# A decay recurrence, its output projection and its group norm put in another order, by halves of the rows

## The chip, the cores and the metric

The kernel runs on one core of one Trainium2 chip. The metric is the time on the device of one execution, in microseconds. The program has five engines with a queue each: PE (TensorE, matmuls), DVE (VectorE), ACT (ScalarE), POOL (GpSimd) and SP (SyncE, which here issues the weight transfers). They meet only in semaphores.

## The reference

Two blocks are computed for 256 rows of 1024 columns. The change lies in the middle of the second one, in a group of eight heads of 64 columns (RWKV-7). Cut to what matters:

```python
def rwkv7_scan(r, decay, k, v, kk, a):
    def step(S, inp):
        r_t, w_t, k_t, v_t, kk_t, a_t = inp
        sa = jnp.einsum('bhij,bhj->bhi', S, -kk_t)
        S = (S * w_t[:, :, None, :] + sa[..., None] * (kk_t * a_t)[:, :, None, :]
             + v_t[..., None] * k_t[:, :, None, :])
        y = jnp.einsum('bhij,bhj->bhi', S, r_t)
        return S, y
...
    y = rwkv7_scan(rh, heads(decay), kh, vh, kk, ah)
    mean = jnp.mean(y, axis=-1, keepdims=True)
    var = jnp.mean(jnp.square(y - mean), axis=-1, keepdims=True)
    y = (y - mean) * lax.rsqrt(var + GN_EPS)
    y = y * lnx_w + lnx_b
    y = (y + bonus) * g
...
    return jnp.concatenate([y_rwkv, y_att], axis=-1) @ w_out
```

The result is added to the rows, normalized, and goes into a feed-forward block.

## The kernel before, in words

The order on every engine is written out by hand. `plan()` only gives each product a PSUM bank (eight banks; `s.use(name, bank)`) and lists the weight units. A weight unit is 1 MB; SP loads it, ACT writes its high part (`split` in ACT's block), DVE its low part, and PE multiplies in three matmuls (`three`): high by high, high by low, low by high. Three units can be split at a time, so the split of a unit waits until PE is done with the one three before. On PE, `take(name)` waits for the bank to be empty and `give(ins, name)` reports it full.

The scan is done in 8 rounds (`NCH`) of 32 rows (`C`). Ahead of it an inverse is computed for four groups `g` of four heads and 128 rows (`INVERSE`; steps GN to ZZ, two groups taking turns); its step Z1 multiplies the inverse with two matrices, `An` and `Z[:, 1]`, 64 columns each.

A round c on PE: `recalled` (the state against WT, 8 matmuls into two banks, one for even heads and one for odd), the state product of Kn and Vn (8 matmuls), one of eight groups of masked products (`PRODUCTS`, four matmuls of heads of one parity; they are for the outputs only), then, once DVE has written SA, the state product of Bn and SA. Even and odd heads have a state bank each (`ste`, `sto`). DVE in a round: decays the old state, one instruction for each parity (64 partitions each); writes SA, one each; adds the new state, one each; masks the 512 columns of products. The next round's `recalled` waits for the new state.

Behind the eight rounds PE computes the outputs of rows 0 to 127 (`y0`) and of rows 128 to 255 (`y1`), each from SA products, Vn products and states. Then comes the group norm of all 256 rows: means (`gm0`, `gm1`, by halves of the columns), DVE's centring, ACT's squares, sums over each head (`gv`), ACT's root, DVE's reciprocal, `unfold_rows` which spreads it to the columns again, and four DVE steps with a copy on ACT between. The output projection has four units: 512 attention rows of `w_out` by 512 columns, twice (48 matmuls of 128x512), and 512 RWKV rows by 512 columns, twice (48 more). The attention half does not need the scan, and PE runs it while DVE and ACT work at the group norm. `row_transposes` then turns the new rows for the feed-forward block.

Lines of the profile: L1967 is `recalled`, L1961 the state products, L1982 the masked products, L2001 and L2011 the outputs, L2017 the means, L1837 the variance, L1847 the unfolding, L1607 to L1609 the three matmuls of `three`, L1708 the row transposes; L1918 to L1932 are the inverse. On DVE L1416 is the decay, L1423 SA, L1429 the state's addition, L1362 a mask, L1441 the centring, L1447 the reciprocal, L1457 to L1466 the four steps, L999 a low part of weights, L1224 the residual. On ACT L613 is a copy out of PSUM, L873 the squares, L875 the root, L880 the high part of the rows, L602 that of weights.

## Time and profile before

| | |
|---|---|
| time of 3 runs, median (lowest, highest) | 1093.39 us (1091.84, 1093.6) |
| the profiled execution | 1094.86 us |
| its span in the trace | 1093.1 us |
| mean granted clock of PE | 0.943 of 2.4 GHz |
| PE busy | 1000.1 us, 91% |
| DVE busy | 580.9 us, 53% |
| ACT busy | 452.9 us, 41% |
| the chain that ended last | PE 85%, DVE 5%, issue 5%, ACT 3% |

The span is the time from the first to the last recorded instruction. Busy is the time in which an engine ran something; a wait for a semaphore is not busy. The record of a matmul contains its way through the array, so in a row of them the distance between starts is what each costs, and "mean ns of one" is longer. An fp32 matmul stands as two records. "128\*64" behind MATMUL is the part of the array that is used, rows by columns. PEclk (granted clock) is 1.00 at 2.4 GHz and 0.50 at 1.2 GHz. In an idle note, [1.01 <-DVE ...] is how long the engine stood still before the group's first instruction, and who released it.

### The profile page before, as it was taken

The page shows a single profiled execution, that of the slowest core. Times are in us where ns is not written, and L with a number is a line of the kernel's source. Part 1 is how long each engine was busy: PE and PEld are TensorE (multiplying, and loading weights), DVE is VectorE, ACT ScalarE, POOL GpSimd, SP SyncE. Part 2 cuts the span into 40 slices and gives each one's busy share as a digit, 9 for nine tenths or more (in the row PEclk, how much of TensorE's full clock was granted, in tenths as well). Part 3 has the DMA queues.
Part 4 walks back from the last instruction along what each step waited for, and adds up shares of the span by engine and source line. Part 5 has one row for each costly group of instructions (what it writes and reads, how often), then busy time and mean ns, then how long its engine had stood idle before and what let it go on. Part 6 is the DMA issues. An engine that isn't in the chain of part 4 may idle for free.

```text
span 1093.1 us, 16977 instructions
## 1 busy us (share of the span) xinstructions
PE 1000.1 (91%) x7278; PEld 889.5 (81%) x7278; DVE 580.9 (53%) x711; ACT 452.9 (41%) x620; POOL 42.9 (4%) x86
## 2 busy tenths in 40 slices
PE   4999999998899995998899999999889589999996
PEld 4898788897698784997778999998877369998995
DVE  4456656456545478344437555556533286555554
ACT  5445554444444563221035444444432255444442
POOL 6000000000110002100000000000100000000000
PEclk9999999999989897897599999999999889999998
DMA  9663344455556231000014565656556145565530
GB/s 307 196 196 118 125 145 135 136 185 183 182 174 184 86 116 39 2 1 1 1 40 150 197 193 174 200 170 199 167 160 176 27 135 165 182 195 191 193 116 39
DMA packets 108714, 152.52 MB, mean 140 GB/s; under 512 B 4050, under 2 KB 86368, under 8 KB 108640
## 3 DMA queue, kind: packets, MB, share of 16 engines
q1 hardware_dynamic: 101120, 141.45, 40.0%
q10 hardware_dynamic: 5296, 4.79, 1.9%
q0 software_dynamic: 2224, 5.20, 1.5%
q8 instruction: 58, 0.95, 0.4%
q14 instruction: 16, 0.13, 0.0%
HBM read 145.58 MB, written 1.06 MB: 134 GB/s over the span
## 4 chain that ended last, share of the span: by engine, by line
PE 85%; DVE 5%; issue 5%; ACT 3%; DMA 1%; POOL 0%; POOLq 0%; SPq 0%; ACTq 0%; DVEq 0%
PE banks L1607 22%; PE banks L1608 22%; PE banks L1609 22%; PE banks L1932 4%; PE banks L2069 3%; PE banks L1982 1%; PE banks L1961 1%; ACT wh L602 1%; PE banks L1736 1%; PE banks L1725 1%; PE banks L1719 1%; PE banks L1718 1%; DMA raw<-in_w_in 1%; PE banks L1967 1%; PE banks L1867 1%
## 5 line engine op out<-in xcount | busy, mean ns | idle before, releaser
L999 DVE TENSOR_TENSOR wl<-raw,wh 128x2048 fp32r<-128x2048 f32 x132 | 302.2, 2291 | 213.7 <-ACT wh L602 212.8
L1607 PE MATMUL banks<-xh,wh 128*128 128x256 f32 x1216 | 345.5, 284 | 2.0 <-DVE xl L1047 1.8
L1608 PE MATMUL banks<-xl,wh 128*128 128x256 f32 x1216 | 342.5, 282 | 0.0
L1609 PE MATMUL banks<-xh,wl 128*128 128x256 f32 x1216 | 342.2, 281 | 0.0
L602 ACT ACTIVATE wh<-raw 128x2048 fp32r<-128x2048 f32 x132 | 252.1, 1911 | 126.0 <-PE banks L1609 121.9
L1607 PEld LDWEIGHTS banks<-xh,wh 128*128 128x128 f32 x1216 | 230.6, 190 | 8.5 <-issue 7.2
L1608 PEld LDWEIGHTS banks<-xl,wh 128*128 128x128 f32 x1216 | 230.3, 189 | 1.3
L1609 PEld LDWEIGHTS banks<-xh,wl 128*128 128x128 f32 x1216 | 230.6, 190 | 0.0
L1607 PE MATMUL banks<-wh,yh 128*128 128x512 f32 x288 | 113.2, 393 | 1.8 <-DVE yl L1466 1.8
L1608 PE MATMUL banks<-wl,yh 128*128 128x512 f32 x288 | 112.2, 390 | 0.0
L1609 PE MATMUL banks<-wh,yl 128*128 128x512 f32 x288 | 112.2, 390 | 0.0
L896 ACT ACTIVATE ytmp<-banks 128x512 f32<-128x512 f32 x32 | 19.1, 598 | 110.1 <-PE banks L1609 110.1
L1607 PEld LDWEIGHTS banks<-wh,yh 128*128 128x128 f32 x288 | 54.1, 188 | 13.0 <-issue 2.8
L1609 PEld LDWEIGHTS banks<-wh,yl 128*128 128x128 f32 x288 | 54.1, 188 | 11.5
L1479 DVE TENSOR_TENSOR ytmp<-ytmp 128x512 f32<-128x512 f32 x32 | 22.2, 693 | 77.5 <-ACT yh L900 77.5
L1608 PEld LDWEIGHTS banks<-wl,yh 128*128 128x128 f32 x288 | 54.1, 188 | 10.3 <-issue 0.2
L613 ACT ACTIVATE arena<-banks 128x512 f32<-128x512 f32 (+1 forms) x51 | 29.7, 593 | 78.2 <-PE banks L1609 40.2
L1607 PE MATMUL banks<-wh,xh 128*128 128x512 f32 x112 | 47.7, 426 | 13.3 <-DVE xl L1559 7.8
L1608 PE MATMUL banks<-wl,xh 128*128 128x512 f32 x112 | 46.5, 415 | 0.0
L1609 PE MATMUL banks<-wh,xl 128*128 128x512 f32 x112 | 46.2, 412 | 0.0
L2069 PE MATMUL banks<-arena,yover 128*32 128x256 f32 x512 | 31.9, 412 | 12.3 <-issue 12.3
L1607 PEld LDWEIGHTS banks<-wh,xh 128*128 128x128 f32 x112 | 22.6, 202 | 19.9 <-issue 14.6
(289 smaller groups left out, 1115.8 us busy)
## 6 DMA issues: line engine op xcount, KB each, us to landing
raw<-in_l_ffn_up SPq DMA_DIRECT2D x32, 1024.0 KB, 5.5
raw<-in_l_ffn_down SPq DMA_DIRECT2D x32, 1024.0 KB, 5.0
raw<-in_w_in SPq DMA_DIRECT2D x29, 1024.0 KB, 5.3
raw<-in_l_w_in SPq DMA_DIRECT2D x13, 1024.0 KB, 5.2
raw<-in_l_pw SPq DMA_DIRECT2D x12, 1024.0 KB, 5.4
arena<-arena ACTq DMA_DIRECT2D x64, 71.0 KB, 3.0
raw<-in_w_out SPq DMA_DIRECT2D x4, 1024.0 KB, 5.1
raw<-in_l_w_out SPq DMA_DIRECT2D x4, 1024.0 KB, 5.0
```

Of the source, the lines that this page charges most:

```text
L602: nc.scalar.activation(wh[:, u % WBUFS, :], raw[:, u % RAWS, :], ACT.Copy).then_inc(E("hi_split"), 1)
L613: nc.scalar.activation(dst, src, ACT.Copy, scale=scale).then_inc(empty(name), 1)
L896: nc.scalar.activation(ytmp[:, k % 2, :], bank(name), ACT.Relu).then_inc(empty(name), 1)
L999: nc.vector.tensor_tensor(wl[:, u % WBUFS, :], raw[:, u % RAWS, :], wh[:, u % WBUFS, :].bitcast(F32), ALU.subtract).then_inc(E("lo_split"), 1)
L1479: mark(nc.vector.tensor_tensor(hid, hid, hid, ALU.mult))
L1607: mm(out, hh, mh, start=start, stop=False)
L1608: mm(out, hh, ml, start=False, stop=False)
L1609: return mm(out, hl, mh, start=False, stop=stop)
L1718: mm(out[:, 0:P], q[:, 0:P], k[:, 0:P], start=True, stop=True)
L1719: give(mm(out[:, P:384], q[:, P:T], k, start=True, stop=True), f"sc{a}")
L1932: ins = mm(o, m(ts[lhs]), m(ts[rhs]), start=True, stop=True)
L2069: ins = mm(out[32 * q:32 * q + 32, j * T:(j + 1) * T], tap_blocks(i)[:, g, 4 * j + q, :], shifted(i)[:, j, q, SHIFTS * g:SHIFTS * g + T], ...
```

## The change

1. The two halves of the state are written into one bank (`st`), and DVE decays and adds them in one instruction each.
2. The masked products are taken in another grouping: in a round four heads, even and odd by turns (`received`), into two banks; DVE masks them in two instructions ahead of the state's addition.
3. In rounds 0 to 3, PE does six matmuls of the first attention unit at the end of a round (`attention_part`). In round 4 it does the states' part of `y0`, in rounds 5 and 6 its two products' parts.
4. The group norm is done for rows 0 to 127 first and for the others behind it, and the projection too: `rwkv_part(c, s)` is 12 matmuls for one half of the rows and of the columns.
5. `An` moves to where `Z[:, 0]` lies, and Z1 is one matmul of 128 columns instead of two of 64.
6. ACT's split of the last projection unit stands ahead of the copy of `y0`.

The core of the diff (some removed lines left out; the code before is above):

```diff
     for c in range(NCH):
         s.use(f"sae{c}", 2), s.use(f"sao{c}", 3)
         if c < NCH - 1:
...
+            s.use(f"st{c}", 1)
+        s.use(f"pre{c}", 0), s.use(f"pro{c}", 7)
+        if c == 0:
+            s.unit("N", "l0_w_out_2", 512, 0, None)
+            s.unit("N", "l0_w_out_2", 512, 512, None)
+            s.use("wp0_0", 4), s.use("wp0_1", 5)
+        elif c == 4:
+            s.use("y0", 6)
+    s.use("gm0", 6)
+    s.use("y1", 1)
+    s.use("gv0", 2)
+    s.use("wp1_0", 6)
+    s.use("gv_b0", 3)
+    s.use("gm1", 0)
+    s.use("wp1_1", 7)
+    s.use("gv1", 2)
+    s.use("gv_b1", 3)
     for c in range(2):
         s.unit("N", "l0_w_out_2", 0, 512 * c, f"wp{c}_1")
 
...
-        An, Bn, Kn, Vn = tiles(slot(8)), tiles(slot(3)), tiles(slot(10)), tiles(slot(11))
+        Bn, Kn, Vn = tiles(slot(3)), tiles(slot(10)), tiles(slot(11))
         Z = oslot(0, 2).rearrange("p (w s h d) -> p w s h d", w=2, s=NT, h=8)
+        An = Z[:, 0, :, :, :].rearrange("p s h d -> p s (h d)")
...
             for i in range(2):
                 copy_out(WT[:, :, i * P:(i + 1) * P], f"wt{i}")
 
...
             next_unit()
...
+            copy_out(YT[:, :, half(0)], "y0")
+            group_squares(0)
+            copy_out(YT[:, :, half(1)], "y1")
+            group_deviation(0)
+            group_squares(1)
+            group_deviation(1)
+            for t in range(NT):
+                act.wait_ge(E("rwkv_out"), t + 1)
+                nc.scalar.activation(yh[:, 0:4, half(t)], centred[:, :, half(t)], ACT.Copy).then_inc(E("rwkv_hi"), 1)
             for _ in range(2):
                 next_unit()
 
...
             for c in range(NCH):
...
+                    if c:
+                        wait_empty(dve, f"st{c - 1}")
+                    mark(nc.vector.tensor_tensor(heads_of(decayed), heads_of(S(c)), pc1, ALU.mult))
...
+                for par in range(2):
+                    use = f"sa{'eo'[par]}{c}"
+                    wait_full(dve, use)
+                    nc.vector.tensor_tensor(heads_of(SA[pb:pb + C, tt, :])[:, par::2, :], heads_of(bank(use)[pb:pb + C, 0:T]),
+                                            Z[pb:pb + C, 1, tt, par::2, :], ALU.add).then_inc(empty(use), 1)
+                upto = const("upinc32").rearrange("p (o t) -> p o t", o=1).broadcast_to([P, 2, P])
+                for par in range(2):
+                    use = f"pr{'eo'[par]}{c}"
+                    wait_full(dve, use)
+                    at = 512 * (c // 2 % 2) + T * (c % 2)
+                    nc.vector.tensor_tensor(products(2 * tt + par)[:, at:at + T].rearrange("p (h t) -> p h t", h=2),
+                                            bank(use)[:, 0:T].rearrange("p (h t) -> p h t", h=2), upto, ALU.mult)\
+                        .then_inc(empty(use), 1)
                 if c < NCH - 1:
...
+                    wait_full(dve, f"st{c}")
+                    sync()
+                    nc.vector.tensor_tensor(S(c + 1), bank(f"st{c}")[:, 0:T], decayed, ALU.add).then_inc(empty(f"st{c}"), 1)
...
+            centre(0)
             next_unit()
+            group_rstd(0)
             dve.wait_ge(E("gates_folded"), 4)
...
+            normalize(0)
+            centre(1)
+            gate_and_shift(0)
+            group_rstd(1)
+            rwkv_low(0)
+            normalize(1)
+            gate_and_shift(1)
+            rwkv_low(1)
             add_residual("wp", units=((), (2,)), norm="f0")
             split_norm("f0", (2, 3))
             next_unit()
...
                             elif name == "Z1":
-                                mm(o[:, 0:HD], m(ts[4]), An[:, tt, h * HD:(h + 1) * HD], start=True, stop=True)
-                                ins = mm(o[:, HD:P], m(ts[4]), Z[:, 1, tt, h, :], start=True, stop=True)
+                                ins = mm(o.rearrange("p (w d) -> p w d", w=2), m(ts[4]), Z[:, :, tt, h, :],
+                                         start=True, stop=True)
...
+            def attention_part(c, s, ks):
+
+                u = UID[("N", "l0_w_out_2", 512, 512 * c)]
+                if s == 0 and ks[0] == 0:
+                    arrived(u)
+                h, l = w_views(u, 512)
+                out = take(f"wp{c}_{s}") if ks[0] == 0 else bank(f"wp{c}_{s}")
+                rows = slice(s * P, (s + 1) * P)
+                for k in ks:
+                    ins = three(out, yh[:, 4 + k, rows], yl[:, 4 + k, rows], h[:, k, :], l[:, k, :], k == 0, False)
+                if s == 1 and ks[-1] == 3:
+                    ins.then_inc(E("unit_summed"), 1)
+
...
+                    ins = three(bank(f"wp{c}_{s}"), yh[:, k, rows], yl[:, k, rows], h[:, k, :], l[:, k, :], False, k == 3)
+                give(ins, f"wp{c}_{s}")
...
+            def first_half_outputs(c):
+                if c == 4:
+                    take("y0")
+                    state_part(0, 0, 4, True)
+                elif c == 5:
+                    product_part(0, SA, 0, False)
+                else:
+                    give(product_part(0, Vn, 512, True), "y0")
+
...
+                def received(p, par):
+                    h = 4 * (c % 2) + 2 * p + par
+                    return mm(outs[par][:, p * P:(p + 1) * P], htile(kTil if c // 2 % 2 else bTil, tt, h), htile(rTil, tt, h),
+                              start=True, stop=True)
+
+                if c:
+                    wait_empty(pe, f"st{c - 1}")
                 outs = [take(f"sa{e}{c}") for e in "eo"]
                 for par, ins in enumerate(both_parities(recalled)):
                     give(ins, f"sa{'eo'[par]}{c}")
                 if c < NCH - 1:
-                    take(f"ste{c}"), take(f"sto{c}")
+                    take(f"st{c}")
                     both_parities(state_mm(Kn, Vn, True))
...
+                outs = [take(f"pr{e}{c}") for e in "eo"]
+                for par, ins in enumerate(both_parities(received, 2)):
+                    give(ins, f"pr{'eo'[par]}{c}")
+                if c < NCH - 1:
+                    wait_empty(pe, f"sae{c}"), wait_empty(pe, f"sao{c}")
+                    give(both_parities(state_mm(Bn, SA, False))[1], f"st{c}")
+                if c < 4:
+                    attention_part(0, c // 2, range(2 * (c % 2), 2 * (c % 2) + 2))
+                elif c < NCH - 1:
+                    first_half_outputs(c)
+
...
+            group_mean(0)
+            take("y1")
+            state_part(1, 0, 4, True)
             wait_empty(pe, f"sae{NCH - 1}"), wait_empty(pe, f"sao{NCH - 1}")
...
+            product_part(1, SA, 0, False)
+            wait_empty(pe, f"pre{NCH - 1}"), wait_empty(pe, f"pro{NCH - 1}")
+            give(product_part(1, Vn, 512, True), "y1")
+            group_variance(0)
+            attention_part(1, 0, range(4))
+            unfold_group(0)
+            group_mean(1)
+            attention_part(1, 1, range(4))
+            group_variance(1)
+            rwkv_part(0, 0)
+            unfold_group(1)
+            rwkv_part(1, 0)
+            rwkv_part(0, 1)
             row_transposes("f0", "wp", 0)
-            nat_unit(("wp1_0", "wp1_1"), 0, yh, yl, turn=1, part=1)
+            rwkv_part(1, 1)
             row_transposes("f0", "wp", 1)
```

On PE, the end of a round and the start of the next, before. L1961 is the state product, L1967 `recalled`, L1982 the masked products; "x7" is seven more of the same:

```order
L1961 MATMUL banks<-arena 64x64 [waits emptied3,emptied2]
L1961 MATMUL banks<-arena 64x64 x7
L1967 MATMUL banks<-extra_t,arena 32x64 [waits emptied2,emptied3,emptied7,emptied4]
L1967 MATMUL banks<-extra_t,arena 32x64 x7
L1961 MATMUL banks<-arena 64x64 [waits emptied7,emptied4]
L1961 MATMUL banks<-arena 64x64 x7
L1982 MATMUL banks<-arena 128x128 [waits emptied0]
L1982 MATMUL banks<-arena 128x128 x3
```

The same place now (end of round 0, start of round 1). L2048 is the state product, L2054 `recalled`, L1641 to L1643 are the three matmuls of a weight unit, here of the attention half:

```order
L2048 MATMUL banks<-arena 64x64 [waits emptied3,emptied2]
L2048 MATMUL banks<-arena 64x64 x7
L1641 MATMUL banks<-wh,yh 128x512 [waits emptied4,lo_split,hi_split]
L1642 MATMUL banks<-wl,yh 128x512
L1643 MATMUL banks<-wh,yl 128x512
L1641 MATMUL banks<-wh,yh 128x512
L1642 MATMUL banks<-wl,yh 128x512
L1643 MATMUL banks<-wh,yl 128x512
L2054 MATMUL banks<-extra_t,arena 32x64 [waits emptied3,emptied2,emptied1]
L2054 MATMUL banks<-extra_t,arena 32x64 x7
L2048 MATMUL banks<-arena 64x64 [waits emptied1]
L2048 MATMUL banks<-arena 64x64 x7
```

Six matmuls of 128x512 have come between the second state product and the next `recalled`.

On ACT, from the copies of WT to the high part of the projection's rows, before. L613 is a copy out of PSUM, L873 the squares, L875 the root, L602 a split of weights:

```order
L613 ACTIVATE arena<-banks 128x4x128 [waits filled1]
L613 ACTIVATE arena<-banks 128x4x128 [waits filled0]
L613 ACTIVATE ytmp<-banks 128x4x128 [waits filled5]
L613 ACTIVATE ytmp<-banks 128x4x128 [waits filled6]
L873 ACTIVATE arena<-arena 128x512 [waits emptied1]
L873 ACTIVATE arena<-arena 128x512 [waits emptied0]
L875 ACT_TABLE_LOAD
L875 ACTIVATE arena<-banks,small 128x256 [waits filled1]
L602 ACTIVATE wh<-raw 128x2048 [waits unit_summed,unit_loaded3]
L880 ACTIVATE yh<-arena 128x512 [waits rwkv_out] x2
```

Now (L622 copy, L611 split of weights, L884 squares, L888 root, L899 high part of the rows):

```order
L622 ACTIVATE arena<-banks 128x4x128 [waits filled1]
L622 ACTIVATE arena<-banks 128x4x128 [waits filled0]
L611 ACTIVATE wh<-raw 128x2048 [waits unit_summed,unit_loaded3]
L622 ACTIVATE ytmp<-banks 128x4x128 [waits filled6]
L884 ACTIVATE yover<-yover 128x4x128 [waits emptied6]
L622 ACTIVATE ytmp<-banks 128x4x128 [waits filled1]
L888 ACT_TABLE_LOAD
L888 ACTIVATE thb<-banks,small 128x128 [waits filled2]
L884 ACTIVATE yover<-yover 128x4x128 [waits emptied0]
L888 ACTIVATE thb<-banks,small 128x128 [waits filled2]
L899 ACTIVATE yh<-yover 128x4x128 [waits rwkv_out] x2
```

The split of weights has moved up; the copy of `y1` stands ahead of the first root, and the second root ahead of the high part of the first rows.

On DVE, from the centring to the low parts, before (L1441 centring, L1447 reciprocal, L999 split of weights, L1457 to L1466 the four steps):

```order
L1441 SCALAR_TENSOR_TENSOR arena<-banks,ytmp 128x512 [waits filled1,emptied5,emptied6]
L1441 SCALAR_TENSOR_TENSOR arena<-banks,ytmp 128x512 [waits filled0]
L1447 RECIPROCAL arena<-arena 128x256 [waits emptied1,emptied0]
L999 TENSOR_TENSOR wl<-raw,wh 128x2048 [waits unit_summed,hi_split]
L1457 TENSOR_TENSOR arena<-arena,banks 128x512 [waits filled0,gates_folded]
L1457 TENSOR_TENSOR arena<-arena,banks 128x512 [waits filled1]
L1460 TENSOR_TENSOR arena<-arena 128x512 [waits emptied0]
L1460 TENSOR_TENSOR arena<-arena 128x512 [waits emptied1]
L1463 TENSOR_TENSOR arena<-arena,over 128x512 [waits dve_steps]
L1463 TENSOR_TENSOR arena<-arena,over 128x512
L1466 TENSOR_TENSOR yl<-arena,yh 128x512 [waits rwkv_hi] x2
```

Now (L1463 centring, L1017 split of weights, L1470 reciprocal, L1476, L1482 and L1484 the steps, L1489 the low part):

```order
L1463 SCALAR_TENSOR_TENSOR yover<-banks,ytmp 128x4x128 [waits emptied6,filled6]
L1017 TENSOR_TENSOR wl<-raw,wh 128x2048 [waits unit_summed,hi_split]
L1470 RECIPROCAL thb<-thb 128x128 [waits emptied2]
L1476 TENSOR_TENSOR yover<-yover,banks 128x4x128 [waits emptied6,filled3,gates_folded]
L1463 SCALAR_TENSOR_TENSOR yover<-banks,ytmp 128x4x128 [waits emptied1,filled0]
L1482 TENSOR_TENSOR yover<-yover,arena 128x4x128 [waits emptied3]
L1484 TENSOR_TENSOR yover<-yover,over 128x4x128 [waits dve_steps]
L1470 RECIPROCAL thb<-thb 128x128 [waits emptied2]
L1489 TENSOR_TENSOR yl<-yover,yh 128x4x128 [waits rwkv_hi]
L1476 TENSOR_TENSOR yover<-yover,banks 128x4x128 [waits emptied0,filled3]
L1482 TENSOR_TENSOR yover<-yover,arena 128x4x128 [waits emptied3]
L1484 TENSOR_TENSOR yover<-yover,over 128x4x128 [waits dve_steps]
```

The second reciprocal stands ahead of the first low part, and everything has 128 rows instead of half of the columns.

## Rows read from the trace of the kernel before

**Rows 1.** PE, timeline of rounds: start, length, line, shape, count, [idle before].

```profile
499.62 0.64 PE L1967 MATMUL banks<-extra_t,arena 64*32 64x64 f32 x16 [0.78 <-ACT arena L613]
500.19 0.68 PE L1961 MATMUL banks<-arena 32*64 32x64 f32 x16
500.80 1.16 PE L1982 MATMUL banks<-arena 64*128 64x128 f32 x8
...
509.74 1.07 PE L1967 MATMUL banks<-extra_t,arena 64*32 64x64 f32 x16 [1.01 <-DVE extra_t L1429]
...
511.78 2.07 PE L1982 MATMUL banks<-arena 64*128 64x128 f32 x8
...
515.90 1.07 PE L1967 MATMUL banks<-extra_t,arena 64*32 64x64 f32 x16 [1.01 <-DVE extra_t L1429]
```

**Rows 2.** PE, timeline of outputs, group norm and projection.

```profile
549.50 1.97 PE L2001 MATMUL banks<-arena 128*64 128x128 f32 x32
...
551.40 2.06 PE L2011 MATMUL banks<-arena,over 64*64 64x32 f32 x64
...
557.36 0.39 PE L1607 MATMUL banks<-wh,yh 128*128 128x512 f32 x1
557.59 0.39 PE L1608 MATMUL banks<-wl,yh 128*128 128x512 f32 x1
...
558.81 0.64 PE L1837 MATMUL banks<-arena,cst 128*32 128x256 f32 x8
559.38 0.50 PE L1607 MATMUL banks<-wh,yh 128*128 128x512 f32 x1
...
559.72 0.39 PE L1608 MATMUL banks<-wl,yh 128*128 128x512 f32 x1
...
571.40 0.47 PE L1607 MATMUL banks<-wh,yh 128*128 128x512 f32 x1 [1.78 <-DVE yl L1466]
...
584.86 0.36 PE L1607 MATMUL banks<-xh,wh 128*128 128x256 f32 x1
```

**Rows 3.** DVE, timeline at the end of a round.

```profile
508.76 0.88 DVE L1429 TENSOR_TENSOR extra_t<-banks,thb 64x256 f32<-64x256 f32 x2 [3.01 <-PE banks L1961]
...
509.67 0.69 DVE L1362 TENSOR_TENSOR arena<-banks,cst 128x512 f32<-128x512 f32 x1
```

**Rows 4.** Windows: busy us of PE, PEld, DVE, ACT, POOL, then PEclk; two of PE alone.

```profile
510.00:520.00 10.00, 8.99 (x98) 7.81 (x93) 4.92 (x12) 0.00 (x0) 0.00 (x0) 0.50 0.01 2
...
550.00:560.00 10.00, 9.26 (x119) 6.79 (x116) 1.38 (x2) 3.83 (x6) 0.00 (x0) 1.00 0.01 2
...
570.00:580.00 10.00, 8.60 (x39) 7.13 (x40) 5.29 (x6) 4.86 (x4) 0.00 (x0) 1.00 0.14 51
...
503.00:504.00 1.00, 0.43 (x9) 0.79 0.00 0
...
547.00:548.00 1.00, 1.00 (x20) 0.53 0.00 0
```

**Rows 5.** PE, timeline at the end of the inverse.

```profile
485.63 2.90 PE L1932 MATMUL banks<-arena 128*128 128x128 f32 x24
...
490.03 0.39 PE L1928 MATMUL banks<-over,arena 128*128 128x64 f32 x2
490.25 0.39 PE L1927 MATMUL banks<-arena 128*128 128x64 f32 x2
```

**Rows 6.** PE, timeline where products of one and of the other row half meet.

```profile
429.35 0.27 PE L1920 MATMUL banks<-over,arena 64*128 64x128 f32 x1
429.35 0.27 PE L1918 MATMUL banks<-over,arena 64*128 64x128 f32 x1
```

**Rows 7.** ACT and DVE, timeline of the group norm and the projection.

```profile
557.56 1.28 ACT L875 ACT_TABLE_LOAD   x1
...
560.13 1.75 DVE L1447 RECIPROCAL arena<-arena 128x256 f32<-128x256 f32 x1 [3.25 <-ACT arena L875]
...
577.76 2.29 DVE L999 TENSOR_TENSOR wl<-raw,wh 128x2048 fp32r<-128x2048 f32 x1
```

213 lines of the change are left out of this document (89 added, 124 removed).

## The prediction

> **What bounds the kernel now.** I read the page first (section 1: PE busy for 91% of the span; section 2: slices 16 to 20 carry a lowered PEclk, almost no DMA and a quiet ACT), then the windows of that stretch, its timeline engine by engine, and the chain of waits. The stretch is the part that the change rewrites: from the first matmul of the recurrence at 499.62 [rows 1] to the first up-projection matmul of the feed-forward block at 584.86 [rows 2], 85.24 us of the 1093.1. Before and after it PE is full of 128x512 and 128x256 matmuls, and nothing of the change touches them.
>
> A round of the recurrence, at the half clock that holds through most of it, is 6.16 us (two starts of L1967 [rows 1]): recalled states and first state product 2.04 together, the masked products' matmuls about 2.0, second state product about 1.1, and 1.01 idle in which DVE adds the new state (two instructions, 0.88 together) and a semaphore goes over. The last product mask (0.69) comes behind that add on DVE [rows 3], so it holds up nobody. PE is busy for 8.99 of 10 us and yet the granted clock is 0.50 there, which is the 1.2 GHz level; in 550 to 560 it is 1.00, 2.4 GHz [rows 4]. The clock fell inside the microsecond 503 to 504, after one round of these small matmuls, and rose inside 547 to 548, when PE had gone over to the outputs' matmuls, which use all 128 rows and two column halves at once [rows 4]. So the stretch pays twice: for waits, and for work at half speed.
>
> **The inverse, before the recurrence.** Two records of 64 columns (L1928, then L1927) lie 0.22 us apart, start to start, and 24 records of 128 columns (L1932) take 2.90 [rows 5]: 0.11 to 0.12 a record either way. The change joins pairs of 64 columns into one of 128: per group of four heads 8 matmuls of two records become 4, 1.78 us becomes 0.89, and there are four groups: 3.6 us saved. PE has no idle time beside those rows. What could eat it is that Z1 of the other group now covers only 0.89 us of ACT's copy (0.60 and two hand-overs, under 0.8); the neighbouring EZ and ZZ steps already run with that cover. I take 3.6, with 2.5 as the low end.
>
> **A round at full clock.** Recalled states 0.57 and first state product 0.61 [rows 1]. The product matmuls (now `received`, still four of two records) took 1.16 together in round 0 [rows 1], all on one half of the rows. In the new order they alternate between row halves. Where such matmuls met before, two records of L1918 and L1920 start at the same 429.35 [rows 6], so they overlap; bounds are 0.45 (8 times half of 0.11) and 1.16, and I take 0.65, since the block also has its start-up. The second state product 0.61. That it writes one bank for both parities costs nothing: the output matmuls of L2001 write one bank from both column halves and still take 0.059 us a record for 128 columns against 0.11 [rows 2, 5]. Sum 2.44.
>
> In rounds 0 to 3 six attention matmuls follow, 0.23 each [rows 2]: 1.38, and 0.15 for going from 32-row to 128-row tiles and back. The nearest row for that is the first 128x512 matmul after the small L1837 block, whose successor follows 0.34 later instead of 0.23 [rows 2], 0.11 more; bounds 0.1 and 0.4. The Trainium skill (TensorEngine Tiling (Array Packing), Key Properties) says that changing the tiling mode drains TensorE; that speaks against mixing kinds like this. No row here prices a drain alone; at the upper bound above it would be 1 us more over the four rounds.
>
> This block hides DVE's state add. DVE now has, after `received`, two half-size masks ahead of the add: 3 instructions of 256 columns, 0.43 each [rows 3], so the new state is there some 1.5 us after `received` ended, and PE has 0.61 + 1.38 to do in that time. If it had nothing, a round would wait 0.9. So rounds 0 to 3: 3.97 each, 15.9. Round 4 has 64 records of state answers (2.0 [rows 2]): 4.4. Rounds 5 and 6 have 16 records of product answers (0.95 [rows 2]): 3.4 each, just as long as DVE's path. Together 27.1 us.
>
> **From round 7 on**, t counted from its start. Recalled, received 1.2; first mean 0.95 (ACT's copy of y0 ended at 0.75); state answers 2.0; product answers 1.9: y1 is complete at 6.05. First variance 0.35 (the 8 records of L1837 with 256 columns took 0.57 [rows 2]), 12 attention matmuls 2.76, to 9.15. Meanwhile ACT: copy of y1, then the table load of 1.28, which before ran beside the projection and now stands between y1 and the first root [rows 7]; root at 8.4, DVE's reciprocal of 128 columns 0.9 (half of 1.75 [rows 7]) to 9.3. Unfold 0.9 (8 records of 128 columns at 0.11), mean 0.9, 12 attention matmuls, variance: t = 14.4.
>
> Here a new wait takes the place of the one before L1607 (1.78 us [rows 2]). `rwkv_part(0, 0)` needs the low part of the first rows. Its input is ready at 13.3, but ACT has the second half's root queued ahead of the high part, and that root waits for PE's second variance at 14.3; DVE has the second reciprocal ahead of the low part. Root 0.4, high part 0.6, reciprocal 0.9, low part 0.65 (ACT and DVE partly beside each other): PE goes on at 16.5, a wait of 2.1. Then 12 projection matmuls, unfold, 12 more: 22.9. The second rows' chain starts only from that unfold (20.15): three DVE steps, ACT's copy, the subtraction, 0.65 each with hand-overs: 23.65, a wait of 0.75. Twelve more to 26.4. The transposes now stand directly behind the block whose residual add they need (before, 12 matmuls lay between): 0.75 wait and 0.7 work. Last twelve to 30.6. DVE must still do a 2.29 us split [rows 7], low parts and two adds before the last transposes: about 2.6, against 1.6 now. First up-projection matmul at t = 33.2.
>
> **Sum.** 27.1 + 33.2 = 60.3 instead of 85.24: 24.9 saved, with the inverse 28.5. This is with 2.4 GHz throughout. In rounds 0 to 3 every 4 us now hold 1.38 us of full-array matmuls, the kind beside which the clock is 1.00 [rows 4], so I take full clock there. Rounds 4 to 7 lose that filling; round 4 is made of the small matmuls beside which it fell. I charge 3 us for a stretch at 1.2 GHz there (the doubled part of about one and a half rounds; bounds 0 and 7). Left: 25.5. The profiled execution was 1094.86 with a span of 1093.1; the median of three is 1093.39, 1.5 lower than the profiled one. I take the saving off the median: 1068.
>
> Busy time alone does not bring the full clock here: 8.99 of 10 us and still 0.50 [rows 4]. The Trainium skill (TensorE: Matmul & The Clock Gate, Part 1) says that the throttle follows how busy PE has been; by that rule the changed rounds, busier still, would all run at 2.4 GHz and the time would be 1065, and the rows just named speak against taking it at its word.
>
> **Rivals.**
> 1. The half clock stays from round 1 to round 7, since three fifths of a round are still small matmuls. For it: busy time did not help before. Against: the rise at 547 came from matmuls no denser than these. Price: the attention matmuls then take 0.43 to 0.46 each, rounds 1 to 3 7.1 each, round 4 6.6, rounds 5 and 6 6.1, round 7 2.1 more: 3.9 + 21.3 + 6.6 + 12.2 + 35.3 = 79.3. Saved 5.9 + 3.6 = 9.5: 1084. 16%.
> 2. The waits go, but the overlap of row halves does not come (received 1.16 in 8 rounds: 4.1 more) and each of some ten changes of tile kind costs 0.4 rather than 0.15 (2.5 more), at full clock: 1075. For it: L1982 took 1.16 rather than 0.88 for 8 records, so starting a block does cost. 18%.
> 3. Slower. PE runs the projection too at 1.2 GHz: its blocks of 12 are now cut by waits of 2.1, 0.75 and 0.75. Each of 72 attention and projection matmuls behind round 7 costs 0.23 more. On top of rival 1, 41 of them use up the 9.5 saved; with all 72, 16.6 is lost and the time is 1100. Against: in 570 to 580 [rows 4] PE works at 1.00 right behind an idle 1.78. 2%.
> 4. The change does not do what it says: the new waits (ACT and DVE queue orders) give back everything. They would have to total 28 us; the whole tail holds four waits of 4 us together. 1%.
>
> **Numbers.** The forecast's case holds 63%, 1063 to 1072; within it the clock's 3 us and the price of `received` move most. Of rivals 1 and 2 the range takes in nearly all that lies below 1082, where part of the rounds runs at half clock. Low end: no loss of clock, and `received` at 0.45, gives 1063.5. Range 1062 to 1082. Faster by over 0.2% (2.2 us, about what a measurement of this kernel can tell): forecast, rivals 1 and 2, 0.96; slower 0.02; within 0.02.
>
> **What would show it.** Right: six attention matmuls at 0.23 spacing behind each of the first four second state products, PE's idle time before L2054 gone, granted clock near 1.00 there; rounds near 4 us; one wait of some 2 us before the first projection matmul, released by DVE's low part; the stretch near 60 to 64 us. Wrong: rounds of 7 us with clock 0.50 (rival 1); `received` blocks of 1.16 us at full clock (rival 2); an idle time of over 4 us between y1 and the transposes, which would mean that I misread a queue; matmuls of the feed-forward block changed in length.

## The result and the profile after

| | before | after |
|---|---|---|
| median of the runs compared, us | 1092.80 (1091.84 to 1093.6) | 1062.91 (1062.19 to 1064.81, 4 runs) |
| profiled execution, time and span, us | 1094.86, 1093.1 | 1062.19, 1060.4 |
| mean granted clock | 0.943 | 0.967 |

The ratio is 0.9716, 95% interval [0.9696, 0.9735]. The forecast was 1068, so the change saved some 4 to 5 us more than forecast, and the time lies 0.9 above the low end of the range. The experiments below ran the changed kernel ten times more, and those runs alter the picture: its executions lie at two levels, near 1062 and near 1073. The four above are all at the lower one.

The timeline of PE in the kernel after, round 0. It answers to [rows 1].

```profile
489.36 0.64 PE L2054 MATMUL banks<-extra_t,arena 64*32 64x64 f32 x16 [0.78 <-ACT arena L622]
489.93 0.68 PE L2048 MATMUL banks<-arena 32*64 32x64 f32 x16
490.54 0.71 PE L2059 MATMUL banks<-arena 64*128 64x128 f32 x8
491.18 0.68 PE L2048 MATMUL banks<-arena 32*64 32x64 f32 x16
491.79 0.50 PE L1641 MATMUL banks<-wh,yh 128*128 128x512 f32 x1
...
493.06 0.39 PE L1643 MATMUL banks<-wh,yl 128*128 128x512 f32 x1
493.38 0.64 PE L2054 MATMUL banks<-extra_t,arena 64*32 64x64 f32 x16
```

A round takes 4.02 (489.36 to 493.38). L2059 (`received`) takes 0.64 to the next start, from 490.54 to 491.18, and its records together 0.71. L1982 had 1.16 for its records [rows 1] and 1.09 to the next start (500.80 to 501.89, below). PE's idle time before `recalled` is gone. The two changes of tile kind can be read from the starts. The first attention matmul's successor follows 0.34 later instead of 0.23, and `recalled` stands 0.32 behind the start of the last one, 0.09 over the usual 0.23: 0.2 in all for going to full tiles and back.

PE, rounds 4 to 7, and the tail up to the first up-projection matmul (550.46), which answers to [rows 2].

```profile
507.86 2.06 PE L2018 MATMUL banks<-arena,extra_t 64*64 64x32 f32 x64
509.85 0.64 PE L2054 MATMUL banks<-over,arena 64*32 64x64 f32 x16
...
513.30 0.64 PE L2054 MATMUL banks<-over,arena 64*32 64x64 f32 x16
...
533.57 0.47 PE L1641 MATMUL banks<-wh,yh 128*128 128x512 f32 x1 [2.11 <-DVE yl L1489]
...
541.04 0.50 PE L1641 MATMUL banks<-wh,yh 128*128 128x512 f32 x1 [0.85 <-DVE yl L1489]
...
549.32 1.39 PE L1742 MATMUL banks<-cst,xn 128*128 128x128 f32 x8 [0.85 <-DVE xn L1242]
550.46 0.36 PE L1641 MATMUL banks<-xh,wh 128*128 128x256 f32 x1
```

The first round of answers costs 4.42 (505.43 to 509.85), the next two 3.45 and 3.46. Line L2018 is the states' part of `y0`. The stretch is 489.36 to 550.46, 61.10 where it was 85.24. The one wait of 2.11 stands before the first `rwkv_part`, and the others are 0.85, 0.56 (before the first transposes) and 0.85. ACT and DVE around the 2.11 (two timelines), which answer to [rows 7]:

```profile
531.52 0.37 ACT L888 ACTIVATE thb<-banks,small 128x128 f32<-128x128 f32 x1 [1.76 <-PE banks L2090]
531.79 0.62 ACT L899 ACTIVATE yh<-yover 128x512 fp32r<-128x512 f32 x1
```
```profile
529.73 0.69 DVE L1484 TENSOR_TENSOR yover<-yover,over 128x512 f32<-128x512 f32 x1
531.92 0.95 DVE L1470 RECIPROCAL thb<-thb 128x128 f32<-128x128 f32 x1 [1.50 <-ACT thb L888]
532.79 0.63 DVE L1489 TENSOR_TENSOR yl<-yover,yh 128x512 fp32r<-128x512 f32 x1
```

The input of the high part is complete at 530.4 (end of L1484). ACT writes it only at 531.79, behind the second root, and DVE's low part (532.79) stands behind the second reciprocal.

Windows of the kernel after, with the columns of [rows 4]: PE, PEld, DVE, ACT, POOL busy, then PEclk, DMA share, GB/s.

```profile
500.00:510.00 10.00, 10.00 (x194) 8.20 (x196) 5.37 (x15) 1.91 (x1) 0.00 (x0) 1.00 0.02 4
510.00:520.00 10.00, 10.00 (x204) 7.99 (x200) 6.50 (x17) 0.73 (x2) 0.00 (x0) 1.00 0.01 2
```

The granted clock, 0.50 there before [rows 4], is 1.00 in every window of 10 us from 490 to 560, rounds 4 to 7 included. This holds for executions of the faster level. `a_third` below, the same kernel at the slower one, has 3.4 us at half clock in rounds 0 and 1 (496 to 502) and again in the projection (542 to 546).

The inverse: the last two groups of Z1 took 3.62 before (489.31 to 492.93) and take 1.89 now (480.79 to 482.68), 1.73 less. Four groups save 3.5.

```profile
480.79 1.16 PE L1961 MATMUL banks<-over,arena 128*128 128x128 f32 x8
...
482.68 2.96 PE L1966 MATMUL banks<-arena 128*128 128x128 f32 x24
```

### The profile page after: what moved, and what is told of

Its sections match the earlier page's. It is cut to its first block, busy times and chain, and to the rows that moved or that the text cites. A ratio compares the mean times of both kernels' runs of the same rounds, so it can differ in the third digit from the quotient of the medians.

```text
span 1060.4 us, 16928 instructions
## 1 busy us (share of the span) xinstructions
PE 971.8 (92%) x7262; PEld 864.4 (82%) x7262; DVE 576.0 (54%) x706; ACT 453.2 (43%) x621; POOL 42.8 (4%) x86
## 4 chain that ended last, share of the span: by engine, by line
PE 84%; DVE 6%; issue 4%; ACT 3%; DMA 1%; POOL 0%; POOLq 0%; SPq 0%; DVEq 0%; ACTq 0%
PE banks L1641 23%; PE banks L1642 22%; PE banks L1643 22%; PE banks L1966 4%; PE banks L2159 3%; ACT wh L611 1%; PE banks L1770 1%; PE banks L1759 1%; PE banks L1753 1%; PE banks L1752 1%; DMA raw<-in_w_in 1%; PE banks L2048 1%; DVE wl L1017 1%; PE banks L1958 1%; DVE arena L1380 1%
## 5 line engine op out<-in xcount | busy, mean ns | idle before, releaser
L1017 DVE TENSOR_TENSOR wl<-raw,wh 128x2048 fp32r<-128x2048 f32 x132 | 302.4, 2292 | 211.2 <-ACT wh L611 210.3
L1641 PE MATMUL banks<-xh,wh 128*128 128x256 f32 x1216 | 346.2, 285 | 2.4 <-DVE xl L1065 2.3
L1643 PE MATMUL banks<-xh,wl 128*128 128x256 f32 x1216 | 343.0, 282 | 0.0
L611 ACT ACTIVATE wh<-raw 128x2048 fp32r<-128x2048 f32 x132 | 252.0, 1911 | 135.2 <-PE banks L1643 131.4
L1641 PEld LDWEIGHTS banks<-xh,wh 128*128 128x128 f32 x1216 | 231.6, 190 | 9.2 <-issue 7.8
L1643 PEld LDWEIGHTS banks<-xh,wl 128*128 128x128 f32 x1216 | 231.6, 190 | 0.0
L1641 PE MATMUL banks<-wh,yh 128*128 128x512 f32 x288 | 113.7, 395 | 3.0 <-DVE yl L1489 3.0
L1643 PE MATMUL banks<-wh,yl 128*128 128x512 f32 x288 | 112.2, 390 | 0.0
L1641 PEld LDWEIGHTS banks<-wh,yh 128*128 128x128 f32 x288 | 54.1, 188 | 14.2 <-issue 2.8
L1643 PEld LDWEIGHTS banks<-wh,yl 128*128 128x128 f32 x288 | 54.1, 188 | 11.7
L622 ACT ACTIVATE arena<-banks 128x512 f32<-128x512 f32 (+1 forms) x49 | 28.6, 593 | 71.0 <-PE banks L1643 40.1
L1641 PE MATMUL banks<-wh,xh 128*128 128x512 f32 x112 | 46.3, 414 | 13.4 <-DVE xl L1595 7.8
L1643 PE MATMUL banks<-wh,xl 128*128 128x512 f32 x112 | 45.4, 405 | 0.0
L1641 PEld LDWEIGHTS banks<-wh,xh 128*128 128x128 f32 x112 | 22.0, 196 | 19.9 <-issue 14.6
```

The lines of the kernel that those rows point to most:

```text
L611: nc.scalar.activation(wh[:, u % WBUFS, :], raw[:, u % RAWS, :], ACT.Copy).then_inc(E("hi_split"), 1)
L622: nc.scalar.activation(dst, src, ACT.Copy, scale=scale).then_inc(empty(name), 1)
L1017: nc.vector.tensor_tensor(wl[:, u % WBUFS, :], raw[:, u % RAWS, :], wh[:, u % WBUFS, :].bitcast(F32), ALU.subtract).then_inc(E("lo_split"), 1)
L1641: mm(out, hh, mh, start=start, stop=False)
L1643: return mm(out, hl, mh, start=False, stop=stop)
```

## Experiments

In the diffs, - is the changed kernel (or the kernel before, where named), + the experiment. Two quantities are used throughout: every execution lists its span and its mean granted clock. Span times clock is called "work" here, and span times (1 - clock) the time lost to the clock. The clock is given to 0.001, so each is good to some 0.5 us.

Both are rough where PE waits at half clock, because a wait for DVE does not get shorter when PE's clock rises. The kernel before shows it on PE (three lines beside [rows 1]):

```profile
501.89 0.68 PE L1961 MATMUL banks<-arena 32*64 32x64 f32 x16
503.57 1.06 PE L1967 MATMUL banks<-extra_t,arena 64*32 64x64 f32 x16 [1.01 <-DVE extra_t L1429]
...
540.57 1.07 PE L1967 MATMUL banks<-over,arena 64*32 64x64 f32 x16 [1.01 <-DVE over L1429]
```

Its round 0, at 2.4 GHz, takes 3.95 (499.62 to 503.57), and rounds 1 to 6 take 6.17 each (503.57 to 540.57). The half clock costs such a round 2.2, and not the 3.08 that half of its length would be. Inside the stretch the timelines are therefore the better measure.

### What the clock gives: the attention matmuls ahead of round 0 (`a_attfront`)

```diff
             wait_empty(pe, "o11")
+            attention_part(0, 0, range(4))
+            attention_part(0, 1, range(4))
             for c in range(NCH):
...
-                if c < 4:
-                    attention_part(0, c // 2, range(2 * (c % 2), 2 * (c % 2) + 2))
-                elif c < NCH - 1:
+                if 4 <= c < NCH - 1:
```

> The 24 attention matmuls of the first four rounds stand in one block ahead of round 0; all else is the changed kernel. Theory (full-array matmuls between the small ones keep the clock at 2.4 GHz): the clock falls to 1.2 GHz in round 0 or 1, rounds without them last about 4.8 instead of 4.0, rounds 4 to 7 about 2 to 2.6 more each, attention in front 5.6: about 1078 to 1081. Rival (the clock holds without them, the gain is hidden waits and overlap): rounds of 3.35, waits of 0.9 bared, 1066.

Measured 1080.25 (1079.94 to 1084.03, 4 runs), ratio to before 0.9892 [0.9875, 0.9909].

```profile
520.00:530.00 10.00, 10.00 (x126) 8.41 (x124) 3.87 (x10) 0.00 (x0) 0.00 (x0) 0.50 0.01 2
```

PE's timeline of the same kernel: the first attention matmul, the starts of rounds 1 to 4, and the first up-projection matmul:

```profile
490.44 0.47 PE L1641 MATMUL banks<-wh,yh 128*128 128x512 f32 x1 [0.78 <-ACT arena L622]
...
499.12 0.64 PE L2056 MATMUL banks<-extra_t,arena 64*32 64x64 f32 x16 [0.56 <-DVE extra_t L1455]
...
502.18 0.95 PE L2056 MATMUL banks<-extra_t,arena 64*32 64x64 f32 x16 [0.56 <-DVE extra_t L1455]
...
506.90 1.06 PE L2056 MATMUL banks<-extra_t,arena 64*32 64x64 f32 x16 [0.53 <-DVE extra_t L1455]
...
511.74 1.06 PE L2056 MATMUL banks<-over,arena 64*32 64x64 f32 x16 [0.53 <-DVE over L1455]
...
567.68 0.36 PE L1641 MATMUL banks<-xh,wh 128*128 128x256 f32 x1
```

The same matmuls in another place cost 17.8 us against the changed kernel beside it (1062.46). In the profiles the stretch takes 77.24 (490.44 to 567.68) instead of 61.10: 16.1 of the 17.7 between the two spans.

Of these 16.1, some 1.8 are lost cover. Attention in front takes 5.61 and an unfilled round 3.06 at 2.4 GHz (499.12 to 502.18), 0.56 of it waiting for DVE's add. That makes 17.85 for the attention and four rounds, where four filled rounds take 16.07. The other 14 are the clock. An unfilled round at 1.2 GHz takes 4.84 (506.90 to 511.74). Windows of 2 us, read one by one, put the clock at 0.50 from 502 to 534, 30.7 us in all, and for 3.4 more at 550 to 554.

The parts of y0 stand in rounds 4 to 6 here too, and PE is busy for 10.00 of 10 us in 520 to 530. Yet the clock does not come back before 534: filling that holds a full clock does not quickly bring it back.

### The clock without the cover: unused matmuls in the kernel before (`b_dummy`)

```diff
 (kernel before, end of rounds 0 to 6; three waits ahead of round 0 are left out here)
...
+                    for k in range(6):
+                        mm(banks[:, 5, :], yh[:, 4 + k % 4, 0:P], wh[:, UID[("N", "l0_w_out_2", 512, 0)] % WBUFS, 512 * (k % 4):512 * (k % 4) + 512], start=True, stop=True)
```

Nothing reads the bank that they write.

> The kernel before with six more matmuls of 128x512 (their result is not used) behind the second state product of each of rounds 0 to 6, 42 in all. Theory (they lift the clock): rounds of 4.5 instead of 6.17, outputs of the first rows 1.7 shorter, 1079 to 1082, faster than before by 11 to 13 us although PE does more. Rival (the clock stays at 1.2 GHz): each round pays 2.6 less the 1.0 wait, 1103.

Measured 1085.13 (1080.83 to 1085.3), ratio 0.9916 [0.9896, 0.9937]: 42 matmuls more, and 8 us faster, where 11 to 13 were expected. PE's timeline (rounds 0, 1 and 7, the first up-projection matmul) and a window:

```profile
500.51 0.64 PE L1970 MATMUL banks<-extra_t,arena 64*32 64x64 f32 x16 [0.78 <-ACT arena L613]
...
504.97 0.64 PE L1970 MATMUL banks<-extra_t,arena 64*32 64x64 f32 x16
...
531.71 0.64 PE L1970 MATMUL banks<-over,arena 64*32 64x64 f32 x16
...
572.60 0.36 PE L1607 MATMUL banks<-xh,wh 128*128 128x256 f32 x1
```
```profile
510.00:520.00 10.00, 10.00 (x147) 8.16 (x145) 7.15 (x17) 0.00 (x0) 0.00 (x0) 1.00 0.02 4
```

Rounds of 4.46 at 1.00, where they were 6.16 [rows 1]. Over the four runs its work is 1038 us, against 1029.6 before, and the time lost to the clock 39 to 47 us, against 61 to 68. Here the clock is separated from the row halves, the order of the group norm and Z1.

The stretch takes 72.09 (500.51 to 572.60), 13.15 less than before: the expected gain came there in full. Stages that neither kernel changes took 3.4 longer in this profile (0.9 ahead of the stretch, 2.5 behind it), where the clock fell at other places.

This run also prices the half clock in the kernel before. From round 7 on it takes 40.89 (531.71 to 572.60), where before took 44.29 (540.57 to 584.86): 3.4 more at the lower clock. With 2.2 in each of six rounds that makes some 16.7 us. So of the 24.1 us by which the change shortens the stretch, 16.7 are the clock and some 7.4 the waits, the overlap and the new order.

### Why rounds 4 to 7 kept the clock (`a_outlate`)

```diff
                 if c < 4:
                     attention_part(0, c // 2, range(2 * (c % 2), 2 * (c % 2) + 2))
-                elif c < NCH - 1:
-                    first_half_outputs(c)
...
-            group_mean(0)
+            for c in range(4, NCH - 1):
+                first_half_outputs(c)
             take("y1")
             state_part(1, 0, 4, True)
+            group_mean(0)
```

> The changed kernel with the three parts of y0 taken out of rounds 4 to 6 and put behind round 7 (first mean behind y1's state answers). My prediction counted rounds 4 to 7 as unfilled and charged 3 us for the clock; in fact the parts of y0 that stand there are matmuls on all rows and columns, like those beside which the clock rose before. Theory: they are what held the clock there. Then, without them, the clock falls in about the second unfilled round (as it did 4 us after the start of the recurrence before), rounds 5 to 7 run at 1.2 GHz (6.1 instead of 3.4 each for two of them, 2 more in round 7), and with the 3.0 us of lost cover (10.2 + 4.1 instead of 11.3) the time is 1070 to 1075. Rival: four filled rounds carry the clock over the rest whatever stands in it: rounds 4 to 6 of 3.4 at a granted 1.00, 3 us for the cover alone: 1065 to 1066.

Measured 1072.99 (1071.52 to 1074.55), ratio 0.9809 [0.9786, 0.9832]. PE's timeline, then a window:

```profile
508.69 0.64 PE L2054 MATMUL banks<-over,arena 64*32 64x64 f32 x16 [0.56 <-DVE over L1455]
...
511.75 1.06 PE L2054 MATMUL banks<-over,arena 64*32 64x64 f32 x16 [0.56 <-DVE over L1455]
...
516.58 1.06 PE L2054 MATMUL banks<-over,arena 64*32 64x64 f32 x16 [0.53 <-DVE over L1455]
...
518.73 3.62 PE L2018 MATMUL banks<-arena,extra_t 64*64 64x32 f32 x64
...
559.79 0.36 PE L1641 MATMUL banks<-xh,wh 128*128 128x256 f32 x1
```
```profile
520.00:530.00 10.00, 10.00 (x166) 8.96 (x165) 1.15 (x2) 1.02 (x2) 0.00 (x0) 0.73 0.01 2
```

The clock falls near 511: round 5, of 3.06, is followed by one of 4.83, and then round 7 and the states' part of y0 (3.62 instead of 2.06) run at 1.2 GHz. Windows of 2 us put 13.6 us at half clock there. The stretch takes 70.24 (489.55 to 559.79), 9.1 more. The cover was counted at 3.0 of it, which leaves some 6 for the clock. The theory holds and the rival (1065 to 1066) falls: the parts of y0 in rounds 4 to 6 are what kept the clock. What about them does it is not separated. They use all rows and both column halves, but they also fill PE's wait of 0.56 in each round; no run fills that wait with small matmuls.

### How much spreading is needed (`a_att01`)

```diff
-                if c < 4:
-                    attention_part(0, c // 2, range(2 * (c % 2), 2 * (c % 2) + 2))
-                elif c < NCH - 1:
+                if c < 2:
+                    attention_part(0, c, range(4))
+                elif 4 <= c < NCH - 1:
```

> The changed kernel with twelve attention matmuls in each of rounds 0 and 1 and none in rounds 2 and 3. Same work. At full clock: rounds 0 and 1 of 5.35, rounds 2 and 3 of 3.4 (DVE's path): 17.5 instead of 16.1, so 1064. Theory (the filling has to be spread; about 4 us of the small matmuls alone bring the clock down): the clock falls in round 3, which takes some 6, and is back during round 4's state answers: 1067 to 1070, and a few microseconds at 0.50 in the windows. Rival (dense work ahead of the small matmuls is enough for the two rounds): 1064 and 1.00 throughout.

Four runs at 1065.4, 1066.49, 1073.77 and 1079.22, median 1070.1, ratio 0.9793 [0.9749, 0.9837]. The profile is of the slowest, at 1079.22.

```profile
510.00:520.00 10.00, 8.88 (x172) 7.65 (x170) 6.15 (x16) 0.39 (x1) 0.00 (x0) 0.77 0.01 4
520.00:530.00 10.00, 10.00 (x142) 8.69 (x140) 3.12 (x8) 0.00 (x0) 0.00 (x0) 0.54 0.01 2
```

Rounds 2 and 3 kept 2.4 GHz, which the rival had; but windows of 2 us show the clock falling at 514, as round 4 began, and back only at 530, in round 6. So each had one half. I had expected the state answers of round 4 to bring it back at once; here it took them and the 16 product answers of round 5 as well. This is one execution. The two fastest lost 37 us to the clock in all, where the changed kernel's faster level loses 35 to 38, so they can't have had such a spell: there the dense work ahead was nearly enough, as the rival said. That spreading is needed is shown for some executions, not for all.

### Single pieces

**The order of `received`** (`a_parity`), even, even, odd, odd instead of by turns:

```diff
-                for par, ins in enumerate(both_parities(received, 2)):
-                    give(ins, f"pr{'eo'[par]}{c}")
+                for par in range(2):
+                    received(0, par)
+                    give(received(1, par), f"pr{'eo'[par]}{c}")
```

> The changed kernel with the product matmuls of a round issued first even, even, then odd, odd, instead of by turns. Theory (turns of the row half let two of them run beside each other: 0.64 a block against 1.16 before): the block takes 0.85 to 1.0, eight rounds cost 2 to 3 us, time 1064.5 to 1065.5. Rival (the shorter block comes from the full clock or the smaller mask): block still 0.64, time as the changed kernel.

1063.63 (1062.38 to 1074.79), ratio 0.974 [0.9695, 0.9786].

```profile
492.24 0.72 PE L2059 MATMUL banks<-arena 64*128 64x128 f32 x8
492.89 0.68 PE L2048 MATMUL banks<-arena 32*64 32x64 f32 x16
```

0.65, as with turns (0.64), and not the 0.85 to 1.0 expected. The turns are not what shortens the block. The full clock isn't either, as L1982 took 1.09 to the next start at 2.4 GHz. That both row halves occur in the block remains as the likely cause, but the products also went from one bank to two, and no run separates these.

**The queue order before the projection** (`a_queue`): on ACT the high part of the first rows ahead of the second root, on DVE the low part ahead of the second reciprocal.

```diff
             group_squares(1)
+            rwkv_high(0)
             group_deviation(1)
-            for t in range(NT): ...
+            rwkv_high(1)
...
-            group_rstd(1)
             rwkv_low(0)
+            group_rstd(1)
```

> The changed kernel with two queue orders turned round: ACT writes the high part of the first rows ahead of the second root, DVE the low part ahead of the second reciprocal. Theory (the 2.11 us wait before the first projection matmul comes from these orders): the wait shrinks to 0.2 to 0.5, the stretch to the first up-projection matmul from 61.1 to 59.3, time about 1060.5 to 1061. Rival (the wait is the chain's own length, or comes back at the next part): stretch within 0.5 of 61.1.

```profile
540.10 0.47 PE L1644 MATMUL banks<-wh,yh 128*128 128x512 f32 x1 [0.49 <-DVE yl L1492]
```
```profile
538.60 0.63 ACT L897 ACTIVATE yh<-yover 128x512 fp32r<-128x512 f32 x1 [0.69 <-DVE yover L1487]
539.67 0.37 ACT L888 ACTIVATE thb<-banks,small 128x128 f32<-128x128 f32 x1 [0.45 <-PE banks L2093]
```

The wait is 0.49 instead of 2.11, and from round 7 on the stretch takes 32.10 instead of 33.70: the 1.6 us are real. The runs (1062.24, 1062.62, 1068.19, 1068.87; ratio 0.9729 [0.97, 0.9757]) miss the expected 1060.5 to 1061. At the faster level work is 1023.5 us against the changed kernel's 1025.1, but the time lost to the clock 37.1 against 35.8, so next to nothing is left there. At the slower level its two are 4 us under the changed kernel's.

**The same with the residual adds and the next weight unit in another order** (`a_best`, `a_best2`):

```diff
             group_deviation(1)
-            for _ in range(2):
-                next_unit()
+            next_unit()
...
-            add_residual("wp", units=((), (2,)), norm="f0")
-            split_norm("f0", (2, 3))
+            add_one(0, 0)
+            next_unit()
+            add_one(0, 1)
+            add_one(1, 0)
+            split_norm("f0", (0, 1))
+            add_one(1, 1)
+            split_norm("f0", (2, 3))
```

> As the one before, and the split of the first up-projection unit is taken out of the end: ACT writes its high part ahead of the second rows' high part, DVE its low part between the two residual adds of the first columns; DVE adds the third residual ahead of the low parts of the normalized rows, and ACT writes high parts for the first half of them ahead of the next weights. Theory: 2.3 us between the last projection matmul and the first up-projection matmul becomes about 1.2; stretch about 58, time 1059. Rival (the later units' splits are now late and the feed-forward block waits for them): no gain over a_queue.

> The same kernel as a_best, once more and with more rounds: ACT's high part of the first rows ahead of the second root, DVE's low part ahead of the second reciprocal (wait before the first projection matmul 0.49 instead of 2.11), and the residual adds in another order with the first up-projection unit split earlier. Expected 1059 to 1061, 2 us under the changed kernel (the 1.6 us of the wait and 0.6 at the last transposes); rival: what it gained the first time lay in the clock of stages that it does not touch, and it comes out at 1062 to 1063.

1059.96 (ratio 0.9691 [0.9662, 0.9719]) and 1061.31 (0.9715 [0.9678, 0.9751]). Of twelve executions nine are at 1057.5 to 1061.8 and three at 1066 to 1071. The median of the nine is 2.5 us under that of the changed kernel's faster level (1059.85 and 1062.38). From round 7 on both profiles take 31.5, 2.2 less than the changed kernel: the expected gain, and this is the fastest version.

### The inverse, and the two levels

`b_z1` is the kernel before with Z1 joined (and `An` moved for it) and nothing else; `a_noz1` is the changed kernel with Z1 in two matmuls (and `An` moved back, not shown):

```diff
-                                ins = mm(o.rearrange("p (w d) -> p w d", w=2), m(ts[4]), Z[:, :, tt, h, :],
-                                         start=True, stop=True)
+                                mm(o[:, 0:HD], m(ts[4]), An[:, tt, h * HD:(h + 1) * HD], start=True, stop=True)
+                                ins = mm(o[:, HD:P], m(ts[4]), Z[:, 1, tt, h, :], start=True, stop=True)
```

> The kernel before with An moved and Z1 as one matmul of 128 columns, nothing else. Theory: 16 matmuls less, 3.55 us less on PE, all of it kept: ratio 0.9967, about 1089. Rival (Z1 now covers too little of ACT's copies, new waits before EZ and ZZ): half of it or less, 1091 and above.

1093.93, twelve executions: five at 1085.3 to 1088.8, seven at 1093.2 to 1095.6; ratio 0.9979 [0.9955, 1.0004]. Its work is 1026.9 us, 2.7 under before's; what it lost to the clock was 57 to 59 us in the five and 65 to 68 in the seven, where before loses 61 to 62 mostly. The median is 5 us over the 1089 expected, and as a measure of Z1's time this is inconclusive; the work, 2.7 less, is not far from the 3.5 of the timelines.

> The changed kernel with Z1 of the inverse as before (two matmuls of 64 columns instead of one of 128), nothing else undone. Theory: four groups of 0.89 us come back, 3.6 us, since PE has no idle time there: ratio to the changed kernel 1.0033, time 1066. Rival (the comparison of before with Z1 alone gave 0.998 with an interval that held 1): the saving is eaten by the time that the clock takes elsewhere, and the time is 1062 to 1063.

1073.74 (1070.02 to 1077.05), ratio 0.9805 [0.9781, 0.983]: 11 us over the changed kernel, and 3.6 were expected. So three more were run side by side: the changed kernel (`a_third`), `a_noz1` again (`a_noz1b`), and the changed kernel with each joined Z1 matmul issued twice (`a_z1twice`), which costs PE as much as the two narrow ones.

> The changed kernel once more, as the neighbour of the next two on the same chip. Span times granted clock (the time that it would take at full clock) 1025, and span times (1 - clock), the time lost to the clock, mostly 35 us, now and then 47: 1062, seldom 1074.

> The changed kernel with Z1 of two matmuls of 64 columns, again. Theory A (Z1 costs 3.6 us of work, and besides it moves where the clock falls in stages that it does not touch): work 1029, lost 42 in most executions, 1071 to 1074, 9 to 11 over its neighbour. Theory B (the first comparison met the chip in a poor hour; Z1 is worth its 3.6 us and no more): some executions lose 35 as the neighbour's do, median 1066.

> The changed kernel with each joined Z1 matmul (128 columns) issued twice: 3.6 us of PE work more, just as much as the two matmuls of 64 columns have, in the other shape. If theory A holds because of the time that passes in the inverse: like a_noz1b, lost 42 and 1071 to 1074. If it is the 64 columns that matter: lost 35, 1065 to 1066. If theory B holds: 1066 for both.

| kernel | executions, us | work, us | lost to the clock, us |
|---|---|---|---|
| before (50 executions beside all experiments) | 1091.5 to 1097.6 | 1029.6 | 62.7 |
| changed, faster level (8 of 14) | 1061.9 to 1064.8 | 1025.1 | 35.8 |
| changed, slower level (6 of 14) | 1071.8 to 1074.6 | 1023.7 | 47.5 |
| Z1 in two (9 of 11) | 1070.0 to 1077.1 | 1029.7 | 41.7 |
| Z1 in two (the other 2) | 1088.7, 1090.9 | 1024.9 | 63.1 |
| Z1 joined, issued twice (6) | 1068.4 to 1077.9 | 1028.2 | 41.9 |

`a_third` had 1062.54 once and 1071.8 to 1074.4 five times, median 1072.45 (ratio 0.9791 [0.9763, 0.982]), where the higher value was expected to be seldom; `a_noz1b` 1074.17, and 1072.64 without its two longest (0.9807 [0.9791, 0.9823], from these four); `a_z1twice` 1070.69 (0.9803 [0.9775, 0.9831]). The same kernel earlier, `a_again`:

> The changed kernel once more. Theory: the stretch from the first recalled matmul to the first up-projection matmul is 61.1 us in every execution, and what the change gained beyond it and Z1 (5.0 us in the two profiled executions) is where the clock happened to come back in stages that the change doesn't touch, so it varies: time 1062 to 1065, and the start of the recurrence may lie 2 us elsewhere. Rival: those 5 us belong to the change (the same places and sizes again): start of the recurrence at 489.4 within 0.3.

1062.46, three of four at the faster level, ratio 0.9748 [0.9709, 0.9786]. The stretch takes 61.2 here. In `a_third` it takes 64.2, so the 61.1 does not hold in every execution. And the kernel before, profiled again:

> The kernel before once more, for its profile. Theory (in stages that the change doesn't touch, how long PE stays at 1.2 GHz after a pause differs from execution to execution): the stretches of low clock at 356, 410 and 760 to 850 have other lengths than in the first profile, the time 1091 to 1098. Rival: the same lengths, so what the changed kernel gained there is its own.

1093.51, span 1091.7. As the theory had it, spells at half clock had other lengths than in the first profile: 3.4 us instead of 10.2 near 360, 6.8 instead of 10.2 near 412, 10.2 instead of 3.4 near 766.

Windows of PE in four profiles (us, PE busy, PEclk, DMA share, GB/s): the kernel after, `a_third`, `a_z1twice`, and before again.

```profile
350.00:370.00 20.00, 17.79 (x101) 0.91 0.32 106
...
460.00:480.00 20.00, 18.39 (x174) 1.00 0.01 2
```
```profile
350.00:370.00 20.00, 17.95 (x85) 0.74 0.31 105
...
460.00:480.00 20.00, 18.39 (x148) 0.83 0.00 1
490.00:510.00 20.00, 18.23 (x249) 0.91 0.01 2
```
```profile
350.00:370.00 20.00, 17.79 (x102) 0.91 0.33 106
...
460.00:480.00 20.00, 18.39 (x161) 0.91 0.00 1
```
```profile
350.00:370.00 20.00, 17.95 (x105) 0.91 0.34 106
```

The levels part at 350 to 370, in a stage where the change edits nothing: 0.91 or 0.74, and before's two profiles have it both ways too (0.74 in the first, 0.91 here). In the changed kernel an execution that goes the long way there has more time at half clock at 408 to 420, 466 to 474, 496 to 502 and 542 to 546 as well, and so loses 47 us. The kernel before lost the clock through most of its stretch whichever way it had come (44.4 us at half clock in both profiles), and its two profiled executions, one each way, are 1.4 us apart. Of its 50 executions 13 lie at 1095.3 to 1097.6 with more time lost; none of those has a profile.

Z1: the work is 3.1 us more with it issued twice and 4.6 with it in two (1028.2 and 1029.7 against 1025.1), around the 3.5 of the timelines. Beyond that the clock: in the eleven profiles with the joined Z1, 460 to 480 reads 1.00 where 350 to 370 reads 0.91 (seven), and 0.83 where that reads 0.74 (four); in the six with the longer Z1 (before twice, `b_dummy`, `a_noz1` twice, `a_z1twice`) it reads 0.91. None of the 17 executions with the longer Z1 lost less than 37 us, and seven of 14 of the changed kernel lost 35 to 36. `a_z1twice` at its best is 1068.4: 3.2 of work and some 3 of clock over 1062. So theory A, that the length of Z1 moves the clock in other stages, is supported, and it is the time in the inverse rather than the 64 columns, since both long forms show it. Its price was too high, though: 9 to 11 us over the neighbour were expected and 0.2 measured (1072.64 and 1072.45), as the neighbour was mostly at the slower level. Theory B's 1066 did not come either. On the mean the changed kernel lost 40.8 us in its 14 executions, Z1 in two 41.7 in its nine and Z1 issued twice 41.9: some 1 us of clock, beside 3 to 5 of work. The 11 us of the first comparison came from four executions at one level. What decides at 355 which way an execution goes stays open, and so do the two executions of `a_noz1b` that lost 63 us, of which there is no profile.

## Why the prediction was right or wrong

- **The mechanism and the full-clock sum: right.** The stretch was put at 60.3 without any loss of clock and took 61.10. Rounds 0 to 3 took 4.02 (forecast 3.97), round 4 4.42 (4.4), rounds 5 and 6 3.45 (3.4), from round 7 on 33.7 (33.2), `received` 0.64 (0.65), the new wait 2.11 (2.1), the later ones 0.85 and 0.56 (0.75 each), and 2.2 from the last projection matmuls to the first up-projection matmul (2.6). The `received` block is right in size; the reason given for it, the two row halves, is not separated from the second bank. Its old price of 1.16 [rows 1] was the length of the records; from start to start it was 1.09.
- **The inverse: right in work.** 3.6 forecast; the timelines give 3.5.
- **The step that failed: "I charge 3 us for a stretch at 1.2 GHz there".** No microsecond of rounds 4 to 7 was at 1.2 GHz. The reason given, "rounds 4 to 7 lose that filling", contradicts what I had read from [rows 2] and [rows 4] two paragraphs earlier: the clock rose at 547 beside the outputs' matmuls, and the change puts just these into rounds 4 to 6. `a_outlate` takes them out, and the loss comes: 13.6 us at half clock. So the charge belonged to a kernel without that part of the change, and there the loss was some 6 us, twice the 3. Without the charge the forecast is 28.5 saved and 1064.9.
- **A second step was too strong: "Before and after it ... nothing of the change touches them".** The profiled spans differ by 32.7: 24.1 in the stretch, 3.5 in the inverse, some 5 elsewhere. Of these 5, 2.4 stem from 350 to 370 (0.74 against 0.91), where before's own second profile reads 0.91, and 2.1 from the first 27 us, where the first matmuls of 128x512 take 0.63 in before and 0.39 after, but 0.63 in `a_best` too: both differ from execution to execution. (The windows read 1.00 in those first 27 us in all three, so that this is the clock is not shown.) The spell near 470 goes with the length of Z1 and, with what else lies between 370 and the stretch, makes 2.2 between the two profiles. Later stages give 1.7 back on balance. The instructions there are untouched, their time is not. These 5 us took the time below the 1063.5 that the prediction had worked out as the least.
- **The forecast and the two levels.** All four runs of the first measurement were at the faster level. Fourteen executions have a mean of 1067.2 and lie at 1062.4 and 1072.9; the 1068 lies between them, and both are in the range of 1062 to 1082. Its size was thus right on the mean partly by chance: the 3 us that I charged to the wrong place is about what the slower level adds on average (6 of 14 times 10.5 is 4.5). That the two cancel is luck. The range took the spread of costs into account and not that of executions.
- **Rivals.** 1 (half clock stays) is refuted by the windows; it is about what `a_attfront` does (1080 measured, 1084 by the rival's sum). 2 (no overlap of row halves, dear changes of tile) falls with 0.64 and 0.2. 3 and 4 did not occur. The price of rival 2 was summed wrongly: "at full clock" it is 1064.9 + 4.1 + 2.5 = 1071.5, and the 1075 has the charge of 3 in it.

By the timelines of the two profiles the change is worth 16.7 us of clock in the stretch, 7.4 of waits, overlap and order, and 3.5 in the inverse; the 5 elsewhere depend on the execution. The two columns of the table (4.5 us of work and 27 of clock) give the clock too much, since they halve the waits for DVE along with the matmuls.

The Trainium skill (TensorE: Matmul & The Clock Gate, Part 1) ties the throttle to how busy PE is. For this change its direction held, as the changed rounds are busier (10.00 of 10 against 8.99); but `a_outlate` had 10.00 of 10 busy in 520 to 530 with 0.73 granted, and `a_attfront` 10.00 with 0.50, so the profile's busy share does not tell the clock here.

## What to carry to other kernels

Read the granted clock by stage before counting waits: where PE reads busy at half clock, independent matmuls on the whole array, spread through the loop, can be worth more than the idle time that they fill (here 16.7 us against some 7), and unused ones show it in one experiment. When work is moved, ask of each piece what it is for the clock where it lands, not only where it leaves. For differences of a few microseconds compare stretches of the timeline, and span times granted clock and the time lost apart, over many executions: four runs of one kernel were all at one level, and five of six in a later comparison at the other.

## What was not expected of the hardware

- 42 unused 128x512 matmuls made the kernel 8 us faster.
- Four products, two on each half of the rows and into two banks, take 0.65 from start to start instead of 1.09, even when the two of one half stand ahead of the two of the other.
- A filling that holds the full clock (the parts of y0 in the changed kernel) left it at half for some 18 us where it had already fallen (`a_attfront`).
- Going from 32- and 64-row tiles to full ones and back cost 0.2 us a round, in a kernel where such changes come twice a round.
- One program on one core has two levels 10.5 us apart, which part in the clock of one stage near 355 us.
